# Weight chunks split between a stage's last two evacuations, and branch GEMMs evacuated behind the attention's step

## The reference, cut to what matters

```python
y = swiglu(rmsnorm(h, ffn1_pre_g[l]), ffn1_w_gu[l], ffn1_w_down[l])
h = h + 0.5 * rmsnorm(y, ffn1_post_g[l])
u = rmsnorm(h, mix_pre_g[l])
proj = u @ w_in[l]                      # q, k, v of three attentions, and gates
...                                     # oa, ob, oc: three attentions
yb = einsum('bsnc,ncd->bsnd', branches, w_branch[l])
gates = sigmoid(gl.reshape(b, s, 3, 1024) + b_gate[l])
merged = sum(gates * yb, axis=2)
h = h + rmsnorm(merged @ w_out[l], mix_post_g[l])
y = swiglu(rmsnorm(h, ffn2_pre_g[l]), ffn2_w_gu[l], ffn2_w_down[l])
h = h + 0.5 * rmsnorm(y, ffn2_post_g[l])
```

## Time and profile before

| | us |
|---|---|
| median of three runs | 1709.75 (1706.80 to 1710.27) |
| the profiled execution | 1710.25 |
| its span, first to last instruction | 1708.4 |
| TensorE busy, of the span | 1602.2 (94%) |
| weight loads | 1318.6 (77%) |
| VectorE busy | 1068.1 (63%) |
| ScalarE busy | 854.1 (50%) |
| GpSimd busy | 121.9 (7%) |
| mean granted TensorE clock | 0.989 of full speed |

### The profile page before, as it was taken

The page is one execution under the profiler, slowest core; times in us unless marked ns, Lnnn a source line. Parts: engine busy times, 40 slices in busy tenths (PEclk is TensorE's granted clock), DMA queues, the critical chain, the costliest instruction groups (busy, mean ns, idle before and its releaser), DMA issues.

```text
span 1708.4 us, 21793 instructions
## 1 busy us (share of the span) xinstructions
PE 1602.2 (94%) x7796; PEld 1318.6 (77%) x7796; DVE 1068.1 (63%) x1792; ACT 854.1 (50%) x1487; POOL 121.9 (7%) x157
## 2 busy tenths in 40 slices
PE   1769989999999999999999999999999999999998
PEld 1557768777888777878778887888878787778886
DVE  5787677666565646567675556565565567665653
ACT  0346536645444555555464445444465655454442
POOL 3011001100000200002100000000020001200000
PEclk9998989999999999999999999999999999999999
DMA  9575257335555563455655555555582453655552
GB/s 279 202 241 188 72 183 232 128 111 182 188 186 191 149 189 117 124 149 158 193 186 184 189 192 177 187 180 197 161 222 87 130 173 117 210 182 189 177 192 76
DMA packets 155336, 293.27 MB, mean 172 GB/s; under 512 B 10214, under 2 KB 23316, under 8 KB 155228
## 3 DMA queue, kind: packets, MB, share of 16 engines
q1 hardware_dynamic: 149312, 276.60, 50.1%
q0 software_dynamic: 4800, 12.29, 3.2%
q10 hardware_dynamic: 1116, 2.99, 0.5%
HBM read 290.77 MB, written 1.06 MB: 171 GB/s over the span
## 4 chain that ended last, share of the span: by engine, by line
PE 79%; DVE 8%; DMA 5%; ACT 3%; issue 3%; POOL 1%; SPq 0%; DVEq 0%; POOLq 0%; ACTq 0%
PE pb L433 75%; PE pb L437 4%; DMA raw<-in_w_in 3%; DVE wl L1290 2%; DVE acc L1287 1%; DMA raw<-in_w_ada 1%; POOL st L2041 1%; ACT wh L803 1%; DVE xt_l L1287 1%; ACT xt_h L803 1%; DVE dg L1284 0%; ACT pb L803 0%; DVE xt_l L1290 0%; DVE h L1287 0%; DVE pb L1293 0%
## 5 line engine op out<-in xcount | busy, mean ns | idle before, releaser
L803 ACT ACTIVATE wh<-raw 128x1024 fp32r<-128x1024 f32 (+1 forms) x484 | 504.9, 1053 | 440.0 <-PE pb L433 375.9
L1290 DVE TENSOR_TENSOR wl<-raw,wh 128x1024 fp32r<-128x1024 f32 (+1 forms) x484 | 579.2, 1216 | 208.0 <-ACT wh L803 204.3
L433 PE MATMUL pb<-wh,xt_h 128*128 128x512 f32 (+2 forms) x1536 | 593.4, 386 | 14.2 <-ACT wh L803 12.2
L433 PE MATMUL pb<-wl,xt_h 128*128 128x512 f32 (+2 forms) x1536 | 585.4, 381 | 19.0 <-DVE wl L1290 18.9
L433 PE MATMUL pb<-wh,xt_l 128*128 128x512 f32 (+2 forms) x1536 | 585.6, 381 | 0.6 <-DVE xt_l L1287 0.4
L433 PEld LDWEIGHTS pb<-wl,xt_h 128*128 128x128 f32 x1536 | 292.1, 190 | 73.9 <-DVE wl L1290 23.9
L433 PEld LDWEIGHTS pb<-wh,xt_h 128*128 128x128 f32 x1536 | 291.8, 190 | 70.5 <-ACT xt_h L803 12.8
L433 PEld LDWEIGHTS pb<-wh,xt_l 128*128 128x128 f32 x1536 | 291.5, 190 | 59.4 <-DVE xt_l L1287 6.5
L433 PE MATMUL pb<-wh,big_h 128*128 128x512 f32 x352 | 138.7, 394 | 0.0
L433 PE MATMUL pb<-wl,big_h 128*128 128x512 f32 x352 | 138.6, 394 | 0.0
L433 PE MATMUL pb<-wh,big_l 128*128 128x512 f32 x352 | 136.7, 388 | 0.0
(11 more groups left out here) (205 smaller groups left out, 1479.0 us busy)
## 6 DMA issues: line engine op xcount, KB each, us to landing
raw<-in_ffn_w_gu SPq DMA_DIRECT2D x176, 512.0 KB, 4.5
raw<-in_w_in SPq DMA_DIRECT2D x148, 512.0 KB, 4.3
raw<-in_ffn_w_down SPq DMA_DIRECT2D x88, 512.0 KB, 3.8
raw<-in_w_ada SPq DMA_DIRECT2D x48, 512.0 KB, 5.5
raw<-in_w_out SPq DMA_DIRECT2D x32, 512.0 KB, 4.0
raw<-in_w_branch SPq DMA_DIRECT2D x24, 512.0 KB, 3.6
raw<-in_w_in SPq DMA_DIRECT2D x8, 416.0 KB, 4.0
G<-in_na_rpb POOLq DMA_DIRECT2D x32, 96.0 KB, 8.5
```

Of the source, the lines that this page charges most:

```text
L433: return e.matmul(o, a, b, start=start, stop=stop)
L803: return e.activation(o, a, func, **kw)
L1290: return e.tensor_tensor(o, a, b, op)
```

## The change

`Stream` gets a second way to hand out chunks. `early(n)` gives those that the coming `take` calls would give anyway, and of them also such as go to a buffer of one of the current group's first n chunks. `gemm` in `act` and `dve` calls it after row tile 0 of a group that has more than one chunk and isn't the first, so between the evacuations of the two row tiles:

```diff
+    def early(self, n):
+
+        due = []
+        while self.next < len(self.plan):
+            split = self.plan[self.next][4]
+            if split is None or split >= self.taken + self.ahead or split - NW >= self.freed + n:
                 break
...
         def take():
-
-            for c in stream.take():
+            split(stream.take())
+
+        def split(chunks):
+
+            for c in chunks:
                 src, kk, n, _, i, ada_ = plan[c]
...
-        def gemm(g, x, nk, n, evac, head=1, tail=1, between=None, mid=None):
+        def gemm(g, x, nk, n, evac, head=1, tail=1, between=None, mid=None, late=False):
             pair_no[0] += 1
             first_bank = 2 * ((pair_no[0] - 1) % 2)
+            left = []
             gs = groups(nk, n, head, tail)
             for gi, group in enumerate(gs):
                 for _ in group:
                     take()
                 for t in range(2):
                     if any(c0 + kk == nk for c0, kk in group):
-                        evac(g, t, banks[first_bank + t][:, 0:n])
+                        if late:
+                            left.append(t)
+                        else:
+                            evac(g, t, banks[first_bank + t][:, 0:n])
                     if gi == 0 and t == 0 and between:
                         between()
+                    if t == 0 and gi and len(group) > 1:
+                        split(stream.early(len(group) - 1))
                 stream.freed += len(group)
                 if mid and gi == 1:
                     mid()
                 for _ in group:
                     side.fill()
                     later.fill()
+                for t in left:
+                    evac(g, t, banks[first_bank + t][:, 0:n])
```

`dve`'s `take` and `gemm` are changed in the same way. The second part is `late`: the evacuation of both tiles is done behind the group's steps of other work. Only the branches ask for it, in `act` and in `dve` (there with `ev_y`):

```diff
-                    gemm((s, "gate", n, n0), XT, 8, 512, ev_gate, mid=turn_o if n0 == 0 else None)
-                    gemm((s, "y", n, n0), XB, 4, 512, nothing)
+                    gemm((s, "gate", n, n0), XT, 8, 512, ev_gate, late=True, mid=turn_o if n0 == 0 else None)
+                    gemm((s, "y", n, n0), XB, 4, 512, nothing, late=True)
-                    gemm((s, "gate", n, n0), XT, 8, 512, ev_gate, mid=turn_o if n0 == 0 else None)
-                    gemm((s, "y", n, n0), XB, 4, 512, ev_y)
+                    gemm((s, "gate", n, n0), XT, 8, 512, ev_gate, late=True, mid=turn_o if n0 == 0 else None)
+                    gemm((s, "y", n, n0), XB, 4, 512, ev_y, late=True)
```

More of the change, by code:

```diff
@@ L196, in take @@
             if split is not None and not (split <= c + self.ahead and split - NW < self.freed):
+                break
+            due.append(self.next)
+            self.next += 1
+        return due
+    def early(self, n):
[3 more added lines that the diff above has]
+            if split is None or split >= self.taken + self.ahead or split - NW >= self.freed + n:
                 break
```

## The result

The changed kernel takes 1694.23 us (median of 5 runs, 1691.31 to 1694.56); the kernel before, timed beside it, 1707.37 (5 runs, 1705.91 to 1710.27). The ratio is 0.9914, interval 0.9902 to 0.9926: faster by 0.7 to 1.0 per cent. Timed twice more it gave 0.9919 and 0.9922. Over all these runs the medians are 1693.5 (16 runs) and 1707.4 (64 runs), 13.9 us apart.

What follows compares the result with a forecast made beforehand. TensorE was taken to set the end almost everywhere from 392 us on. Seams 5.8, between the blocks 0.3, layer seam 1.5 and part two 4.1 sum to 11.7: 1710.25 - 11.7 = 1698.6, own range 1695 to 1702, wide 1694 to 1706.

Steps and rivals of the forecast that it cites:

- a seam's 1.16: Each seam between block 2's stages: gain 1.16 us, bounds 0.5 and 1.64, leaving an `xt_l` hole of about 0.5.
- the mixers' openings: Start of the mixers in block 2: DMA-bound, could eat two of the five seam gains; counted as nothing.
- the layer seam: Between block 1's layers, the 3.77 us wait for `wh`: gain 1.5 us, from a range of 1.2 to 2.9.
- Part one, the five seams: Block 2's seams between stages: one `wl` split earlier shrinks TensorE's hole; five seams give 5.8 us.
- the late second evacuation: Block 1's layer seam: an early `wl` of about 1.0 us makes the second evacuation 0.5 late.
- Part two: Mixers in block 2: `mkt` holes of 1.62 and 0.88 us go, plus 1.56 for the clock; sum 4.1.
- 1.56 of it, the low clock: Behind layer 0's `mkt` hole in branch 0: eight matmuls at low clock cost 1.56 us, counted as gained.
- The hole does not come back: Rival at block 2's seams: the hole returns and the 5.8 us is lost, time 1704.4; chance 0.15.
- The insertion holds the evacuation up: Rival at the five seams: each split delays the second evacuation by 1.0 us, time 1709.4; chance 0.11.
- The slower case: Rival in the mixers' branches: late evacuations starve TensorE, 2.97 us at each of ten pairs, time 1728.3; chance 0.07.
- The clock did fall elsewhere: Rival on the clock: falls once as before and twice at a new place, 3 x 1.56, time 1703.3; chance 0.07.

Runs made afterwards that it cites:

- The deferral: The changed kernel with two `wl` splits at all seams moved behind the second tile's norm's `xt_l`: 1698.94 us, ratio 0.995 to the kernel before.
- part two only: The kernel before with only the branch GEMMs' evacuations put behind the attention's step, splits as before: 1703.6 us, ratio 0.997.

## Why the prediction was wrong, and what in it was right

The mechanism was right in both parts, and the time came out 4.4 us below the forecast. What failed is the sizing, at two steps. The sum was taken from the profiled run's 1710.25 as if that were the kernel's time, and it is 2.8 us above the median of 64 runs. And the terms were too small: a seam's 1.16 measured 1.35, and the mixers' openings and the stretch of block 1 behind the layer seam, counted as nothing, were not nothing.

**The base: a run above the median.** The sum was made against 1710.25, and over 64 runs the kernel before has a median of 1707.4. The profiled run had the clock fall of 1.56 us in branch 0, which half of the traces with that hole lack, and its block 2 begins the latest of the four traces with its block 1 (392.7 us, the others 388.3 to 391.0). So 2.8 of the 4.4 us are the base's; as a difference of medians 11.7 was forecast and 13.9 came.

**Part one, the five seams: mechanism right, term too small.** All that was said of the order is in the rows. Of 1.16 a seam it gave 1.35, so 6.75 for 5.8. I wrote that the next stop is the `xt_l` of the second row tile, "1.16 us earlier than 583.18". But 583.18 was not the end of VectorE's queue. The three `wl` ended at 579.56 + 3.49 = 583.05, and `xt_l` then stood for ScalarE's `xt_h`, which waited for transposes that the hole itself had made late. ScalarE's row of before:

```profile
582.52 2.18 ACT L803 ACTIVATE xt_h<-pb,cols 128x128 fp32r<-128x128 f32 x8 [2.15 <-PE pb L437]
```

With the hole gone `xt_l` starts as soon as VectorE is free, at 577.63 + 4.20 = 581.83 in the time of before: 1.35 earlier.

**The mixers' openings: counted as nothing, 0.95 in the two profiled runs.** I took them as bound by DMA whatever happened. The deferral shows that the loads there hang on when the splits give buffers back. But the size is uncertain: the `mqt` wait of layer 0 was 0.80 to 1.22 us in the five traces without part one in block 2. With it, it was 0.63, 0.65 and 0.52 in the changed kernel's three, and 0.45, 0.91 and 1.02 in three others with the same seams. Over both layers the means of these traces differ by 0.7.

**Block 1: the layer seam was right, the stretch behind it was not in the sum.** 1.5 was forecast for the seam and 1.4 came in the profile. (The ends of 1.2 and 2.9 are 1.1 and 3.0 by the prediction's own times, 253.31 less 252.2 and less 250.3.) The hole gave 2.1, and 0.7 was lost ahead of it. Of that 0.4 is the late second evacuation, where I had 0.5: `th` starts at 228.53, where 229.09 less the 0.95 of shift is 228.14. The other 0.3 is transposes run at the low clock; the kernel with part two only loses them too. The 1.45 at 300 to 345 us goes with a low-clock stretch that changes its place. I had counted clock falls only at the places where the changed waits are, and as a loss, and gave no reason for leaving the rest of block 1 out.

**Part two: sum right, one term lucky.** 4.1 came in the profile; 1.56 of it, the low clock, is there in three of six traces. Its mean is about 3.3.

With the means of all traces in place of the two profiled ones, the measured terms are 6.75 for the seams, 0.7 for the openings, 3.3 for part two and 2.75 for block 1. That is an estimate of 13.5 us, where the medians differ by 13.9. Of the 16.0 between the two profiled runs, some 2 are chance.

**The rivals.** The hole does not come back: all five seams are won in every trace with VectorE's early `wl` in block 2. The insertion holds the evacuation up only with a second `wl`. The slower case did not come: no wait for `wl` or `wh` shows in a branch, and the late evacuations other than the first make no difference beyond 0.6 us. I didn't look for the lead at which they would. The clock did fall elsewhere, as a gain in eight traces of twelve.

## What to carry to other kernels

Before an instruction's start is taken as its queue's end, look whether the engine was free before it: a start that the removed hole itself made late moves with the hole. A step that frees a buffer is also the order for a load: moving two splits 2.6 us later cost a wait 3.1 us longer at a stage that the DMA engines bound, though VectorE and ScalarE were busy there for less than half the time. Where traces of one program differ by more than the effect, pair each instruction with itself over several traces. Make the sum against the median of the runs, and not against the one that was profiled.

## What the runs showed of the hardware

The low clock is partly chance at one and the same place. Behind the same wait of 1.62 us, after the same work, the granted clock was 0.50 in three traces and 1.00 in three. In block 1 it was low at differing places between 83 and 176 us. The start of block 2 varied from 385.7 to 391.7 us over the six traces whose block 1 is the changed kernel's, where block 2 of the changed kernel repeats to 0.6. The 64 runs of the kernel before have a standard deviation of 2.0 us; that it comes mostly from these places is likely, and not shown. Nor is the loss fixed to a place: eight traces had a low stretch near 302 us and none near 329, and came out some 1.45 us ahead at 345; four had a longer one near 302 and one near 329, and lost 1.5.

The Trainium skill ("TensorE: Matmul & The Clock Gate", "What's actually happening") has the level decided over a window that runs free of the program, and says that the point of the change varies by run for that reason. The three and three behind the one hole agree. The runs show beside it that the length of a hole does not decide alone, and that without the hole no trace of eleven was low there.
